# Moving an expert's down chunks between its gate chunks, with the next expert's rows turned before the clamps, in a routed-experts kernel

## What is computed

```python
logits = xf @ w_router + b_router            # 512 tokens, 32 experts, top 4 each
for each expert e, for its tokens x:
    hu  = x @ w_gate_up[e] + b_gate_up[e]    # w_gate_up[e]: 1024 x 2048
    a   = minimum(hu[:, :1024], 7.0)
    lin = clip(hu[:, 1024:], -7.0, 7.0)
    act = a * sigmoid(1.702 * a) * (lin + 1)
    y  += g * (act @ w_down[e] + b_down[e])  # w_down[e]: 1024 x 1024
```

## Time and profile before

| What | Number |
|---|---|
| median of 3 runs | 1281.37 us |
| the profiled execution | 1282.38 us, its span 1280.6 us |
| TensorE (PE) busy | 1265.1 us, 99% of the span, 13814 matmuls |
| DVE, ACT, POOL busy | 585.0, 184.2, 317.4 us |
| granted clock | 0.997, that is 2.4 GHz |
| DMA | 450.31 MB, mean 352 GB/s, 406 to 422 GB/s in the slices of the expert loop |
| chain that ended last | PE 96%, DVE 2%, ACT 1%, DMA 1% |

### The profile page before, as it was taken

The page is one execution under the profiler, slowest core; times in us unless marked ns, Lnnn a source line. Parts: engine busy times, 40 slices in busy tenths (PEclk is TensorE's granted clock), DMA queues, the critical chain, the costliest instruction groups (busy, mean ns, idle before and its releaser), DMA issues.

```text
span 1280.6 us, 32819 instructions
## 1 busy us (share of the span) xinstructions
PE 1265.1 (99%) x13814; PEld 846.1 (66%) x13814; DVE 585.0 (46%) x984; ACT 184.2 (14%) x279; POOL 317.4 (25%) x319
## 2 busy tenths in 40 slices
PE   8999999999999999999999999999999999999997
PEld 7867777844676766766666556656576666667664
DVE  7776666555433333333333333333333333444345
ACT  4243443410000000000000000000000000000002
POOL 2035533011333332222222222222222222222220
PEclk9999999999999999999999999999999999999999
DMA  9222117589999999999999999999999999999994
GB/s 261 73 66 66 66 67 269 237 325 406 411 414 413 410 419 418 417 420 412 412 416 414 414 416 421 416 419 418 422 420 416 419 418 416 419 418 416 417 398 169
DMA packets 95377, 450.31 MB, mean 352 GB/s; under 512 B 12208, under 2 KB 37280, under 8 KB 45936
## 3 DMA queue, kind: packets, MB, share of 16 engines
q1 hardware_dynamic: 84288, 430.47, 82.2%
q0 software_dynamic: 9568, 18.97, 5.7%
q10 hardware_dynamic: 1488, 0.40, 0.1%
HBM read 439.54 MB, written 18.67 MB: 358 GB/s over the span
## 4 chain that ended last, share of the span: by engine, by line
PE 96%; DVE 2%; ACT 1%; DMA 1%; issue 0%; DVEq 0%; SPq 0%; ACTq 0%
PE gu_bank L1830 50%; PE bank L1844 21%; PE bank L1847 5%; PE bank L1597 5%; PE bank L1599 4%; PE bank L1598 4%; PE first_gu_bank L1830 2%; PE bank L1681 1%; PE bank L1695 1%; PE bank L1658 1%; DMA x_sb<-in_x_dram 1%; PE bank L1806 1%; DVE probs_a L1192 0%; PE fin_bank L1915 0%; PE bank L1615 0%
## 5 line engine op out<-in xcount | busy, mean ns | idle before, releaser
L1830 PE MATMUL gu_bank<-raw,xT 128*32 128x512 f32 x2976 | 331.7, 592 | 0.0
L1830 PEld LDWEIGHTS gu_bank<-raw,xT 128*32 128x32 f32 x2976 | 189.4, 110 | 130.4 <-issue 39.6
L1461 DVE TENSOR_TENSOR gate_in<-gu_bank,b_gu 128x768 f32<-128x768 f32 x31 | 29.7, 958 | 528.6 <-PE gu_bank L1830 528.6
L651 POOL DMA_INDIRECT x_got<-xn_rows,gather_list x96 | 114.5, 1193 | 341.7 <-DVE xT L1472 308.4
L1830 PE MATMUL gu_bank<-raw_c,xT 128*32 128x512 f32 x1488 | 172.1, 592 | 0.0
L1844 PE MATMUL bank<-raw_a,aT 128*32 128x256 f32 x2232 | 170.5, 379 | 0.0
L1847 PE MATMUL bank<-raw_a,aT 128*32 128x256 f32 x744 | 165.6, 379 | 0.0
L1844 PEld LDWEIGHTS bank<-raw_a,aT 128*32 128x32 f32 x2232 | 119.8, 110 | 36.5 <-issue 2.8
L1830 PEld LDWEIGHTS gu_bank<-raw_c,xT 128*32 128x32 f32 x1488 | 94.9, 110 | 65.2 <-issue 19.8
L937 ACT ACTIVATE sig_in<-gate_in 128x768 f32<-128x768 f32 x32 | 27.0, 845 | 641.0 <-DVE gate_in L1465 615.9
L1844 PE MATMUL bank<-raw_b,aT 128*32 128x256 f32 x1152 | 98.4, 380 | 0.0
(11 more groups left out here) (285 smaller groups left out, 1667.2 us busy)
## 6 DMA issues: line engine op xcount, KB each, us to landing
raw<-in_w_gate_up_dram SPq DMA_DIRECT2D x128, 1024.0 KB
raw_c<-in_w_gate_up_dram SPq DMA_DIRECT2D x62, 1024.0 KB
raw_a<-in_w_down_dram SPq DMA_DIRECT2D x62, 1024.0 KB
raw_b<-in_w_down_dram SPq DMA_DIRECT2D x32, 1024.0 KB
raw_e<-in_w_gate_up_dram SPq DMA_DIRECT2D x31, 1024.0 KB
raw_d<-in_w_down_dram SPq DMA_DIRECT2D x31, 1024.0 KB
raw_b<-in_w_gate_up_dram SPq DMA_DIRECT2D x30, 1024.0 KB
raw<-in_w_in_dram SPq DMA_DIRECT2D x24, 512.0 KB, 6.1
```

The costliest lines, as they stand in the source:

```text
L651: pool.indirect_dma_start(out=x_got[:, r, :], out_offset=None, in_=xn_quarters, in_offset=bass.IndirectOffsetOnAxis(ap=gather_list[:, r:r ...
L1461: dve.tensor_tensor(gate_in[:, :, :], gu[:, :, 0:QUARTER], gate_b, ALU.add)
L1830: ins = pe.matmul(gu[c * GROUP:(c + 1) * GROUP, r, :], x[:, i, r * GROUP:(r + 1) * GROUP], w[:, c], start=first, stop=last)
```

## The change

- TensorE runs, in jobs 1 to 30, gate 0 to 5, down 0 and 1, gate 6 and 7, down 2 and 3. SP loads the chunks in that order; the ring, the bytes and the number of loads stay the same, and the numbers m of the chunks follow the new order.
- DVE takes the sums out of PSUM (`take_gu`), turns and scales the next rows, and only then clamps.
- In the last job (31) TensorE keeps the old order, gate 4 to 7 and then down 0 to 3, and DVE's part of that job stands behind the loop as `last_job`, without `turn_got` and `gain_got`. The loads of that job still come in the new order.

```diff
+        GU_AT, DN_AT = (0, 1, 2, 3, 4, 5, 8, 9), (6, 7, 10, 11)
         def gu_chunk(n, i):
-            return i if n == 0 else n * JOB - DN_CHUNKS + i
+            return i if n == 0 else n * JOB - DN_CHUNKS + GU_AT[i]
         def dn_chunk(n, i):
-            return n * JOB + 2 * GU_CHUNKS + i
+            return (n + 1) * JOB - DN_CHUNKS + DN_AT[i]
...
 # SP, job()
-                for i in range(first, GU_CHUNKS):
+                for i in range(first, HEAD):
                     load_gu(e, i, gu_chunk(n, i), b, turns)
-                for i in range(DN_CHUNKS):
-                    load_dn(before_e, i, dn_chunk(n - 1, i), b, turns)
+                for half in range(2):
+                    for i in range(HEAD + 2 * half, HEAD + 2 * half + 2):
+                        load_gu(e, i, gu_chunk(n, i), b, turns)
+                    for i in range(2 * half, 2 * half + 2):
+                        load_dn(before_e, i, dn_chunk(n - 1, i), b, turns)
...
 # SP, before the loads of sum_rows
-            used = fixed(sp, later(gu_chunk(FIRST - 1, GU_CHUNKS - 1) + 1, count, BODY * JOB))
+            used = fixed(sp, later(dn_chunk(FIRST - 2, DN_CHUNKS - 1) + 1, count, BODY * JOB))
...
 # DVE
-                clamp(j, later(gu_chunk(n, GU_CHUNKS - 1) + 1, b, BODY * JOB))
+                take_gu(j, later(gu_chunk(n, GU_CHUNKS - 1) + 1, b, BODY * JOB))
                 turn_got(j + 1, gathered)
                 gain_got(turned)
+                clamp(j)
                 gate(j)
                 turn_act(j, done)
                 take_y(j - 1, done[-1])
+            def last_job(n, b):
+                j = job_no(dve, n, b)
+                gu_loads = fixed(dve, j * 16 + 16)
+                dve.wait_ge(b_gu_loaded, gu_loads)
+                done = [fixed(dve, later(gu_chunk(n, 0) + GU_CHUNKS + i + 1, b, BODY * JOB)) for i in range(DN_CHUNKS)]
+                spread_gu()
+                take_gu(j, later(gu_chunk(n, 0) + GU_CHUNKS, b, BODY * JOB))
+                clamp(j)
+                gate(j)
+                turn_act(j, done)
+                take_y(j - 1, done[-1])
             job(1)
             count = bodies(dve)
-            with dve.Fori(0, count) as b:
-                for n in range(FIRST, FIRST + BODY):
-                    job(n, b)
+            whole = dve.snap(count - 1)
+            with dve.Fori(0, whole) as b:
+                job(FIRST, b)
+            last_job(FIRST, whole)
...
 # TensorE
+            def two_gates(n, first, turns):
+                for i in range(first, first + 2):
+                    m = gu_chunk(n, i)
+                    gate_up(m, i, turns[m // RAW])
+            def two_downs(n, first, j, turns):
+                if first == 0:
+                    pe.wait_ge(aT_ready, fixed(pe, j * DN_CHUNKS))
+                    if n > 1:
+                        pe.wait_ge(y_taken, j - 1)
+                for i in range(first, first + 2):
+                    m = dn_chunk(n - 1, i)
+                    down(m, i, turns[m // RAW])
+            def rest_of_job(n, j, turns):
+                two_gates(n, HEAD, turns)
+                two_downs(n, 0, j, turns)
+                two_gates(n, HEAD + 2, turns)
+                two_downs(n, 2, j, turns)
+            def rest_of_last_job(n, j, turns):
+                two_gates(n, HEAD, turns)
+                two_gates(n, HEAD + 2, turns)
+                two_downs(n, 0, j, turns)
+                two_downs(n, 2, j, turns)
...
-            rest_of_job(FIRST, job_no(pe, FIRST, whole), turns_of(pe, whole))
+            rest_of_last_job(FIRST, job_no(pe, FIRST, whole), turns_of(pe, whole))
```

More of the change, by code:

```diff
@@ L305, in build @@
         ONCE = 7
+        HEAD = GU_CHUNKS // 2
         def place(m):
@@ L1449, in spread_gu, with take_gu @@
                 dve.stream_shuffle(b_gu[:, :, :], b_row[:, :, :], [0] * GROUP).then_inc(b_gu_spread, 1)
-            def clamp(j, used):
+            def take_gu(j, used):
                 dve.wait_ge(b_gu_spread, j + 1)
@@ L1463, in clamp @@
                    .then_inc(gu_taken, 1)
+            def clamp(j):
                 dve.wait_ge(gu_taken, j + 1)
@@ L1524, in _ @@
             gain_got(1)
-            clamp(0, GU_CHUNKS)
+            take_gu(0, GU_CHUNKS)
+            clamp(0)
             gate(0)
@@ L1869, in _ @@
                     sum_lists()
-            HEAD = GU_CHUNKS // 2
             def head(n, j, turns):
@@ L1882, in head @@
                     gate_up(m, i, turns[m // RAW])
-            def rest_of_job(n, j, turns):
-                for i in range(HEAD, GU_CHUNKS):
+            def two_gates(n, first, turns):
+                for i in range(first, first + 2):
                     m = gu_chunk(n, i)
                     gate_up(m, i, turns[m // RAW])
[L1888 to L1891, removed]
+            def two_downs(n, first, j, turns):
[4 more added lines that the diff above has]
+                for i in range(first, first + 2):
                     m = dn_chunk(n - 1, i)
                     down(m, i, turns[m // RAW])
+            def rest_of_job(n, j, turns):
[8 more added lines that the diff above has]
+                two_downs(n, 2, j, turns)
             assert BODY == 1
```

## The result

The changed kernel takes **1287.87 us** (median of 5 runs, 1285.57 to 1289.38) against 1281.32 for the kernel before in the same comparison (5 runs, 1279.21 to 1281.72): 1.0055 times as long, 95% interval 1.0044 to 1.0066. Slower by 6.5 us. The prediction was 1279.8 with a range up to 1281.8, so the sign is wrong. The profiled execution took 1289.38, its span is 1287.6.

What follows compares the result with a forecast made beforehand. TensorE was taken as the bound (99% of the span), losing 0.23 us a job to gathers beside down chunks; the 6.3 saving, capped by a slow DMA engine at 1.6, gave 1281.37 - 1.6 = 1279.8, range 1274.7 to 1281.8.

Steps and rivals of the forecast that it cites:

- Where the gather falls: GpSimd's gathers move from beside down chunks to beside gate chunks: 30 jobs x 0.23 = 6.9 at most, 6.3 taken.
- Rival C: In the job loop, the late `w_used` belongs to down chunks or DVE's transpositions, so the loss stays: 1281.4; chance 0.10.
- The next rows in time: Before each job's first gate chunk: DVE has `x_gained` ready behind only two down chunks, 0.16 early; cost 0.
- Rival D: First gate matmul of each job: `x_gained` too late for PE's sequencer, 0.35 x 30 = 10.5 lost, 1285.6; chance 0.12.
- Rival D's lead of 0.65: PE's sequencer reaches the wait 0.65 before the gate matmul; if all were needed, 0.35 a job.
- The cap: End of the loop: once TensorE gains the margin it waits for weights from one slow DMA engine; gain limited to 1.6.
- forecast A: Near the end, weight loads on a slow DMA engine cap the gain: 1279.8, own range 1278.7 to 1280.5; chance 0.50.
- the margin at the very end is 0.9 to 2.2: Time in us between the last weights landing and TensorE beginning the last down chunk, in the kernel before.
- Rival B: Loads in timed runs aren't slower than TensorE, so no cap and the whole saving comes through: 1275.1; chance 0.28.
- The last job keeps the old order ... 0. SP's new order of loads is TensorE's order.: Last job and SP's loads: keeping TensorE's old order there and reordering the loads were each costed at 0.
- some tenths: Early jobs: the part of the 6.9 saving left to the list stores, so 6.3 was taken.

Runs made afterwards that it cites:

- experiment 9: Kernel before, with GpSimd's three gathers held back until the four down chunks of the job before are done: 1281.2 us, ratio 1.0004.
- the light pair: Kernel before with half of each down chunk left out of the job loop's loads, without and with the gathers held back: ratios 1.0002 and 0.9957.
- experiment 4: Kernel before with half of each down chunk left out of the job loop's loads, TensorE's work the same: 1282.42 us, ratio 1.0002.
- experiment 11: Kernel before with the gathers held back beside gate chunks and half of each down chunk left out of the loads: 1274.81 us, ratio 0.9957.
- experiment 7: Changed kernel with both clamps ahead of the next rows again, DVE's order of before: 1304.2 us, ratio 1.0183.
- experiment 6: Changed kernel with the last job's loads in TensorE's order and the list stores of jobs 2 to 5 held back to gate chunks: 1280.39 us, ratio 1.0005.
- the light kernels: Half of each down chunk not loaded: kernel before with gathers held back, 0.9957; changed kernel with last loads in order and list stores held back, 0.9951.
- experiment 10: Changed kernel with the list stores of jobs 2 to 5 held back, the last job's loads left out of TensorE's order: 1287.84 us, ratio 1.0058.
- experiment 1: Changed kernel with the last job's loads issued in TensorE's order (gate 4 to 7, then down 0 to 3): 1286.41 us, ratio 1.0035.
- experiment 3: Changed kernel with half of each down chunk left out of the job loop's loads, TensorE's work the same: 1283.18 us, ratio 1.0013.
- experiment 5: Changed kernel once more, unaltered, on another chip than its first comparison: 1292.42 us, ratio 1.0095.
- experiment 12: Changed kernel with last job's loads in TensorE's order, list stores held back, half of each down chunk left out of the loads: 1273.72 us, ratio 0.9951.
- experiment 2: Kernel before with the last job's loads in the changed kernel's order while TensorE keeps its old order: 1285.88 us, ratio 1.0035.
- experiment 8: Kernel before with the gathers held back one job too long by a mistake in the edit, so TensorE waits for rows: 1628.88 us, ratio 1.2736.

## Why the prediction was wrong

**Where the gather falls: right.** It named 6.3 to 6.9 for TensorE alone. The job takes 30.96 in the changed kernel, in experiment 9 by the gathers alone, and the light pair gives 5.8 by time. The new place of the gathers is at the head, in the first trace after from

```profile
348.89 1.25 POOL L657 DMA_INDIRECT x_got<-xn_rows,gather_list  x1 [8.66 <-DVE xT L1481]
```

with gate chunk 0 at 349.73, so that the second and the third stand beside gate chunks. Rival C (the loss stays) is out. A gather does slow TensorE, by whatever path; the path itself stays open. The Trainium skill, "SBUF — State Buffer", section "Who interferes with whom", says that PE and ACT never wait on anyone, which gave that rival its chance; the 0.23 a job of experiments 4 and 11 decides against using it here.

**The next rows in time: right.** DVE's timeline after, beside the earlier trace rows:

```profile
344.75 0.96 DVE L1467 TENSOR_TENSOR gate_in<-gu_bank,b_gu 128x768 f32<-128x768 f32 x1 [18.16 <-PE gu_bank L1854]
...
346.48 1.60 DVE L1481 STREAM_TRANSPOSE xT<-x_got 128x768 f32<-128x768 f32 x1
348.11 0.96 DVE L1487 TENSOR_TENSOR xT<-xT,g_ffn 128x768 f32<-128x768 f32 x1
```

The gain is done at 349.07. PE's timeline, from which I had worked out 0.16 to spare, has the first gate matmul start at 349.52 (the chain's 349.73 leaves out its overlap with the ones before); with the answer of 0.10 measured in experiment 7 it had 0.35 to spare. The order of DVE's instructions is as predicted. Rival D's lead of 0.65 isn't needed. But the cover is as thin as I called it: in experiment 6 DVE starts 0.81 late in four jobs, and each loses 0.47, which is 0.81 less this 0.35; experiment 7 shows the full price.

**The cap: the mechanism right, its margin too large.** TensorE meets the loads at about 987, and the jobs then take 31.9, where I wrote over 31.2 in the last third. Experiments 6 and 9 are the cases to which forecast A applies, with the gathers cured and the last job's loads in order (the 3.4 that experiment 6 lost early came off its waits), and they stand 0.2 and 0.8 over the kernel before, where A had 1.6 under it. The term "the margin at the very end is 0.9 to 2.2" was mis-sized: the lower ends of the two intervals leave at most 0.5 and 0.6. The rows say why it is so small. Jobs held by the loads take 31.9, longer than the 31.19 of the kernel before, so that at this pace its loads fall behind too, by about 0.7 a job. In the changed kernel a gate load lands 8.5 after its issue at 318 to 400, 13.6 at 500 to 600, 21.5 at 700 to 800 and about 26 at 900 to 980, and TensorE waits from 28 on; 8.5 + 29 x 0.7 is 29, an estimate by which the kernel before ends just where it would begin to wait. Rival B's premise (loads in timed runs keep up) is out as well, while its number is confirmed when it is made true: 0.9951 and 0.9957 of the kernel before, against 1275.1 / 1281.37 = 0.9951. What the light kernels show is that the loads are the limit; that it is the slowest of the sixteen engines, and not the mean, was read from the earlier trace rows and not tried by itself.

**The step that failed:** "The last job keeps the old order ... 0. SP's new order of loads is TensorE's order." The second sentence is true of jobs 1 to 30 and false of job 31, whose loads come in the new order while TensorE keeps the old one; my own description of the change said so, and I costed it at nothing. It is worth 4.7 of wait and 2.3 to 3.0 of clock, 7.0 to 7.7 in traces; the ratios of experiments 10 and 6 give 6.8. The two parts of the argument should have met: I had just worked out that there is no lead left at the end of the loop, and a load two places late costs nothing only while there is a lead of two places.

**A second miss, smaller and not certain to appear.** I let "some tenths" stand for the list stores and moved only the gathers and scatters in my mind. The split puts down chunks under the four list stores of jobs 2 to 5. Four of the five traces with stores there lost 8.1 to 8.9 in those jobs (experiments 1, 3, 5 and 7; the first trace of the change lost nothing). With full loads the cap gives about half of it back: experiments 5 and 10 differ by 0.0037 in ratio, 4.7 us, and the light pair of experiments 3 and 12 by 0.0062, 7.9 us (these two differ in the last job's loads as well, but neither waits for one). What makes an execution sensitive to them is open.

**The sum, made again:** 6.5 less for TensorE, all of it taken back by the loads; 7.0 to 7.7 for the last job; 0 to 5 for the list stores. That is 7 to 12 over the kernel before, and 6.5 and 12.2 were measured. Rival D was the only one on the slower side and had another cause, so the chances for the sign had no case that held what happened.

## What to carry to other kernels

When a consumer and the queue that feeds it are reordered, write both orders out for every job, the first and the last above all; a peeled job that keeps the old order needs the old order of loads too. The depth of the ring doesn't cover a mismatch at the end of a stretch in which the loads are the limit, for there the lead is used up. And when a piece of work is moved under another, list every DMA that another engine issues at that time, the rare ones of the early jobs as well, not only those that recur.

## What the runs showed of the hardware that wasn't expected

- **A wait can cost clock on top, but not in proportion.** Behind 4.7 us of standing still the granted clock was 0.50, and 48 matmuls took 7.42, 8.03 and 8.17 in three traces instead of 5.15. Behind 2.9 us (experiment 2) it stayed at 1.00, and they took 5.36. Behind waits of about 9 us (experiment 8) the clock cost 1.5 to 3.1 each, no more than behind 4.7.
- **Loads fall behind slowly.** At 418 GB/s and a share of 1.02 TensorE ran undisturbed for 21 jobs, while the time from issue to landing grew from 8.5 to 28 us, and met the loads only near 987; a kernel whose TensorE is 0.7% faster is then held at the loads' pace, and a gain early in the loop comes out as waits late in it.
- **An indirect DMA of GpSimd can cost TensorE time beside matmuls of 256 columns**, about 0.23 a job for the gathers, at full load and with half of each down chunk left out alike (experiments 4 and 11), and up to 2.5 a job for four list stores (experiment 1); in some traces it costs nothing. Beside matmuls of 512 columns it mostly costs nothing, but in experiment 6 four stores there held DVE's next step back by 0.8.
